# Gate tiles, gate sigmoids and stick-breaking heads placed elsewhere in the attention ticks of a two-block layer stack

## The reference, cut to what matters

```python
# block 1 (twice)
y_a = forgetting_attention(q_a, k_a, v_a, f_a + b_forget)      # 6 heads, "fox"
y_b = stick_breaking_attention(q_b, k_b, v_b)                  # 5 heads, "sb"
y_c = dsa_attention(q_c, k_c, v_c, q_i, k_i, w_i)              # 5 heads, "dsa": top 64 keys by 4 index heads
g_a, g_b, g_c = jnp.split(jax.nn.sigmoid(gates), 3, axis=-1)   # gates = part of h @ w_in, 3 x 1024 wide
x = x + (g_a * (y_a @ w_up_fox) + g_b * (y_b @ w_up_sb) + g_c * (y_c @ w_up_dsa)) @ w_out
# block 2 (twice)
mixed = jax.nn.sigmoid(gate_a) * y_swa_projected + jax.nn.sigmoid(gate_b) * y_moba_projected   # 8 + 8 heads
x = x + gt1 * (mixed @ w_out)
```

## Time and profile before

| | us |
|---|---|
| median of 3 runs (lowest, highest) | 2136.32 (2134.76, 2137.23) |
| the profiled execution's own time | 2141.54 |
| its span from first to last instruction | 2139.8 |
| PE busy in the span | 2025.4 (95%) |
| DVE busy | 1469.8 (69%) |
| ACT busy | 975.3 (46%) |
| mean granted TensorE clock | 0.950 of full |

### The profile page before, as it was taken

The page is one execution under the profiler, slowest core; times in us unless marked ns, Lnnn a source line. Parts: engine busy times, 40 slices in busy tenths (PEclk is TensorE's granted clock), DMA queues, the critical chain, the costliest instruction groups (busy, mean ns, idle before and its releaser), DMA issues.

```text
span 2139.8 us, 35812 instructions
## 1 busy us (share of the span) xinstructions
PE 2025.4 (95%) x13668; PEld 1862.9 (87%) x13668; DVE 1469.8 (69%) x2602; ACT 975.3 (46%) x1466; POOL 36.9 (2%) x72
## 2 busy tenths in 40 slices
PE   6999999889999999999989997998899979898998
PEld 6999998879999999998879996897799968887997
DVE  7776558677766776458578776765766668566665
ACT  5335455543344344455644344554444445534443
POOL 0000000000000000000000000000000000000000
PEclk9999999899998999999799998996899989989999
DMA  8774443257763774443247762531345544223453
GB/s 307 269 264 176 177 158 119 89 188 279 280 236 140 276 283 183 163 166 122 68 178 265 276 230 85 199 115 36 135 177 188 195 149 156 109 79 128 177 192 131
DMA packets 76906, 382.15 MB, mean 179 GB/s; under 512 B 8960, under 2 KB 9088, under 8 KB 55552
## 3 DMA queue, kind: packets, MB, share of 16 engines
q1 hardware_dynamic: 67392, 329.78, 42.6%
q0 software_dynamic: 9408, 50.90, 7.0%
HBM read 379.60 MB, written 1.05 MB: 178 GB/s over the span
## 4 chain that ended last, share of the span: by engine, by line
PE 84%; DVE 10%; ACT 4%; issue 2%; DMA 1%; SPq 0%; DVEq 0%; ACTq 0%
PE psum L544 26%; PE psum L545 26%; PE psum L546 26%; DVE weights_low_a L1315 2%; ACT weights_high_a L989 1%; PE psum L867 1%; PE psum L839 1%; DVE h_low L1366 1%; PE psum L637 1%; PE psum L752 1%; PE psum L841 1%; PE psum L635 1%; PE psum L840 1%; DVE weights_low_b L1315 1%; PE psum L743 1%
## 5 line engine op out<-in xcount | busy, mean ns | idle before, releaser
L544 PE MATMUL psum<-h_high,weights_high_a 128*128 128x256 f32 x2480 | 713.9, 288 | 14.6 <-DVE h_low L1362 6.5
L545 PE MATMUL psum<-h_low,weights_high_a 128*128 128x256 f32 x2480 | 706.2, 285 | 0.0
L546 PE MATMUL psum<-h_high,weights_low_a 128*128 128x256 f32 x2480 | 705.6, 285 | 0.0
L1315 DVE TENSOR_TENSOR weights_low_a<-raw_a,weights_high_a 128x2048 fp32r<-128x2048 f32 (+1 forms) x232 | 459.9, 1983 | 109.7 <-ACT weights_high_a L989 107.1
L544 PEld LDWEIGHTS psum<-h_high,weights_high_a 128*128 128x128 f32 x2480 | 479.5, 193 | 29.8 <-issue 12.2
L545 PEld LDWEIGHTS psum<-h_low,weights_high_a 128*128 128x128 f32 x2480 | 480.4, 194 | 7.1 <-issue 1.0
L546 PEld LDWEIGHTS psum<-h_high,weights_low_a 128*128 128x128 f32 x2480 | 479.7, 193 | 0.0
L989 ACT ACTIVATE weights_high_a<-raw_a 128x2048 fp32r<-128x2048 f32 (+1 forms) x232 | 386.8, 1667 | 163.5 <-PE psum L546 144.0
L1315 DVE TENSOR_TENSOR weights_low_b<-raw_b,weights_high_b 128x1024 fp32r<-128x1024 f32 x224 | 273.4, 1221 | 78.9 <-ACT weights_high_b L989 77.9
L989 ACT ACTIVATE weights_high_b<-raw_b 128x1024 fp32r<-128x1024 f32 x224 | 237.6, 1061 | 162.4 <-PE psum L546 162.4
L544 PE MATMUL psum<-weights_high_b,gated_high 128*128 128x512 f32 x608 | 241.1, 396 | 0.0
(11 more groups left out here) (283 smaller groups left out, 2848.0 us busy)
## 6 DMA issues: line engine op xcount, KB each, us to landing
ada_weights<-in_w_ada POOLq DMA_DIRECT2D x64, 768.0 KB, 5.0
raw_a<-in_w_ffn_a_a SPq DMA_DIRECT2D x44, 1024.0 KB, 6.7
raw_a<-in_w_ffn_b_a SPq DMA_DIRECT2D x44, 1024.0 KB, 6.9
raw_a<-in_w_ffn_a SPq DMA_DIRECT2D x64, 512.0 KB, 4.1
raw_b<-in_w_ffn_b SPq DMA_DIRECT2D x64, 512.0 KB, 3.4
raw_a<-in_w_proj_a SPq DMA_DIRECT2D x28, 1024.0 KB, 5.8
raw_a<-in_w_gate_a SPq DMA_DIRECT2D x26, 1024.0 KB, 4.9
raw_b<-in_w_ffn_a_b SPq DMA_DIRECT2D x44, 512.0 KB, 3.5
```

Source lines behind the costliest of these rows:

```text
L544: pe.matmul(out, l_hi, r_hi, start=start, stop=False, skip_group_check=True)
L545: pe.matmul(out, l_hi, r_lo, start=False, stop=False, skip_group_check=True)
L546: return pe.matmul(out, l_lo, r_hi, start=False, stop=stop, skip_group_check=True)
L1315: dve.tensor_tensor(wlo[kind][:, p, 0:width], raw[kind][:, p, 0:width], whi[kind][:, p, 0:width].bitcast(F32), ALU.subtract).then_inc(lo_r ...
```

## The change

Five things are changed.

1. Block 1 runs four stick-breaking heads at items 2, 3, 6 and 7; the six fox heads come after the index heads, the fifth stick-breaking head after them, the dsa heads stay last. The top-64 rounds move from ticks 10 to 15 to ticks 12 to 18, two rounds of the wide half at a time.
2. A table `GATE_TICKS` says in which tick a gate tile is made. In block 1 these are ticks 0 to 26 without 17, 19 and 23; in block 2 they are 0 to 10, 15, 17, 19, 21 and 23. Weight splits that went with a tick now go with the number of the gate tile.
3. The tanh of the gates and both table loads leave the ticks and stand at the start of ACT's up stage, with weight splits between them.
4. The split of the a part of the second up slot leaves the ticks as well: on ACT it stands behind the first tanh, on DVE ahead of the first merge.
5. DVE masks the new scores of item t before it finishes the y of item t-4.

```diff
 def schedule1():
-    items = [("ckv", 0), ("kv", 0), ("fox", 0), ("fox", 1), ("turn", 0), ("turn", 1)]
+    items = [("ckv", 0), ("kv", 0), ("sb", 0), ("sb", 1), ("turn", 0), ("turn", 1), ("sb", 2), ("sb", 3)]
     items += [("idx", h) for h in range(IDX)]
     items += [("turn", 2), ("turn", 3)]
-    items += [("fox", h) for h in range(2, FOX)]
-    items += [("sb", h) for h in range(SB)] + [("dsa", h) for h in range(DSA)]
+    items += [("fox", h) for h in range(FOX)]
+    items += [("sb", 4)] + [("dsa", h) for h in range(DSA)]
...
+GATE_TICKS = {1: [t for t in range(27) if t not in (17, 19, 23)],
+              2: list(range(11)) + [15, 17, 19, 21, 23]}
...
+                    if items[back][0] == "ckv":
+                        pe.wait_ge(now().forget_rows_ready, 2)
...
             def ticks(l, blk, items, gates, walk, n0):
-                first_tanh = len(items) + 3 - KD
...
-                for tick in range(max(len(items) + 3, gates)):
+                for tick in range(len(items) + 3):
+                    g = gate_of(blk, tick)
                     item_copy(blk, items, tick - 3)
                     stick_exp(items, tick - 1)
-                    if tick < gates and tick % 3 == 0:
-                        split_high(l, blk, 1, n0 + tick // 3 + 1)
+                    if g is not None and g % 3 == 0:
+                        split_high(l, blk, 1, n0 + g // 3 + 1)
...
-                    if tick < gates:
-                        gate_tile(blk, walk, tick, gates)
-                        if tick % 3 == 1 or (blk == 2 and tick == 15):
-                            split_high(l, blk, 0, n0 + tick // 3 + 2)
+                    if g is not None:
+                        gate_tile(blk, walk, g)
+                        if g % 3 == 1 and g < gates - 2:
+                            split_high(l, blk, 0, n0 + g // 3 + 2)
...
-                    if tick == first_tanh - 1:
-                        act.preload_act_table_set("exp_and_others")
-                    if first_tanh <= tick < first_tanh + KD:
-                        gate_tanh(blk, tick - first_tanh)
-                act.preload_act_table_set("natural_log_exp_and_others")
...
             def up_and_out(l, blk, n0):
-                for n in range(n0, n0 + 6):
+                act.preload_act_table_set("exp_and_others")
+                gate_tanh(blk, 0)
+                split_high(l, blk, 0, n0 + 1)
+                for f in (1, 2):
+                    gate_tanh(blk, f)
+                split_high(l, blk, 1, n0 + 1)
+                for f in (3, 4):
+                    gate_tanh(blk, f)
+                split_high(l, blk, 0, n0 + 2)
+                for f in (5, 6, 7):
+                    gate_tanh(blk, f)
+                act.preload_act_table_set("natural_log_exp_and_others")
+                for n in range(n0 + 1, n0 + 6):
...
             def ticks(l, blk, items, gates, n0):
-                for tick in range(max(len(items) + 4, gates + 1)):
+                for tick in range(len(items) + 4):
+                    g, before = gate_of(blk, tick), gate_of(blk, tick - 1)
                     item_late(items, tick - 1)
-                    item_y(blk, items, tick - 4)
                     if tick < len(items) and items[tick]:
                         item_early(blk, items, tick)
+                    item_y(blk, items, tick - 4)
...
                 1: {3: tokens1_latent,
-                    10: lambda: top_rounds(0, 3), 11: lambda: top_rounds(0, 3), 12: lambda: top_rounds(0, 2),
-                    13: lambda: top_rounds(1, 3), 14: lambda: top_rounds(1, 3),
-                    15: lambda: (top_rounds(1, 2), finish_selection())},
+                    12: lambda: top_rounds(0, 3), 13: lambda: top_rounds(0, 3), 14: lambda: top_rounds(0, 2),
+                    15: lambda: top_rounds(1, 2), 16: lambda: top_rounds(1, 2), 17: lambda: top_rounds(1, 2),
+                    18: lambda: (top_rounds(1, 2), finish_selection())},
...
                 g = g1 if blk == 1 else g2
+                split_low(l, blk, 0, n0 + 1)
```

More of the change, by code:

```diff
@@ L220, in schedule2, with gate_of @@
     return items
+GATE_TICKS = {1: [t for t in range(27) if t not in (17, 19, 23)],
+              2: list(range(11)) + [15, 17, 19, 21, 23]}
+def gate_of(blk, tick):
+    return GATE_TICKS[blk].index(tick) if tick in GATE_TICKS[blk] else None
 HEADS = ("fox", "sb", "dsa", "swa", "moba")
@@ L848, in ticks @@
                     pe.wait_ge(now().gain_copied, 2)
-                for tick in range(max(len(items) + 3, gates)):
-                    if tick < gates:
-                        gate_tile(l, blk, walk, tick)
+                for tick in range(len(items) + 3):
+                    g = gate_of(blk, tick)
+                    if g is not None:
+                        gate_tile(l, blk, walk, g)
                     if tick < len(items) and items[tick]:
@@ L1179, in item_copy, with gate_tile @@
                                ACT.Copy).then_inc(now().pt_copied, 1)
-            def gate_tile(blk, walk, tick, gates):
-                mark = walk.mark[tick]
+            def gate_tile(blk, walk, g):
+                mark = walk.mark[g]
                 act.wait_ge({"a": now().used[0], "b": now().used[1], "g": now().group_done}[mark[0]], mark[1])
-                act.activation((g1 if blk == 1 else g2)[:, tick, :], ps[:, tick % 2, 0:SEQ],
+                act.activation((g1 if blk == 1 else g2)[:, g, :], ps[:, g % 2, 0:SEQ],
                                ACT.Copy).then_inc(now().gate_copied, 1)
@@ L1602, in ticks @@
             def ticks(l, blk, items, gates, n0):
-                for tick in range(max(len(items) + 4, gates + 1)):
+                for tick in range(len(items) + 4):
+                    g, before = gate_of(blk, tick), gate_of(blk, tick - 1)
                     item_late(items, tick - 1)
-                    item_y(blk, items, tick - 4)
                     if tick < len(items) and items[tick]:
                         item_early(blk, items, tick)
-                    if tick < gates and tick % 3 == 0:
-                        split_low(l, blk, 1, n0 + tick // 3 + 1)
-                    before = tick - 1
-                    if 0 <= before < gates and (before % 3 == 1 or (blk == 2 and before == gates - 1)):
+                    item_y(blk, items, tick - 4)
+                    if g is not None and g % 3 == 0:
+                        split_low(l, blk, 1, n0 + g // 3 + 1)
+                    if before is not None and before % 3 == 1 and before < gates - 2:
                         split_low(l, blk, 0, n0 + before // 3 + 2)
```

6 lines of the change are left out of this document (3 added, 3 removed).

## The result

| | before | after |
|---|---|---|
| median of 4 runs (lowest, highest), us | 2135.54 (2133.36, 2137.23) | 2120.75 (2118.35, 2122.68) |
| span of the profiled execution | 2139.8 | 2116.7 |
| mean granted TensorE clock | 0.950 | 0.967 |

The ratio is 0.9933, 95% interval 0.9919 to 0.9948: 14.8 us faster, where 14.3 were forecast (2122 against 2136.32). So from here on stages are compared, each with its granted clock.

The account below looks back on a forecast made before the run. Bounds taken: PE work in block 1's ticks, small-step chains and low clock in block 2's last ticks. Block 1 +5, block 2 -24, block 1's clock +4.5 gave -14.5 us: 2122 on the median of 2136.32, range 2098 to 2137.

Parts of the forecast that it names:

- Block 2's ticks: Block 2's ticks: moving four gate tiles late gives -11.7 + 1.3 + 0.4 = -10.0 us a layer.
- the walk: Tick-by-tick reckoning with profiled durations: 12.8 us of PE waits in block 1's ticks, block 2's last stage about 32.5 us.
- Rival C: Block 2's last ticks: clock stays at 1.2 GHz because waits between late tiles hold it down; 2144 us, chance 0.10.
- four tiles enter the last ticks for 0.4 us: Block 2's last ticks: four added gate tiles nearly all fill PE waits, lengthening the stage by only 0.4 us.
- Rival E: Block 2's last ticks: late tiles lie on the chain, costing 2 of 2.93 us each; 2138 us, chance 0.15.
- Block 1's ticks: Block 1's ticks: 100.7 us work, 12.8 waits, 0.6 for the last y, 114.1 against 113.1: +1.0 us a layer.
- the term for the clock: Block 1: gaps in ticks 5 and 17 each bring a half-clock spell, three more in all at 1.5 us: +4.5.
- Rival B: Block 1's ticks: the new PE waits don't arise, ticks near 102 us; total 2095.5 us, chance 0.20.
- turn_y: The turn_y stage gets shorter through a higher clock: -0.5 us a layer in block 1, -0.7 in block 2.
- Block 2's up stage: Block 2's up stage starts at full clock, partly offset by the added split on DVE: -1.3 us a layer.
- Block 1's up stage: Block 1's up stage: the split ahead of DVE's first merge, where DVE is nearly the bound, adds +2.0 us a layer.
- rival D: Start of the four up stages: each table load delays the first merge another 1.28 us, 5.1 in all; 2127, chance 0.05.

## Why the prediction was right, and where it was not

**The total** was met, 2122 against 2120.75, and so was the course: faster. That it was met so closely is luck. Block 1 was forecast at +9.5 us (+5, and +4.5 for its clock), and between the two profiled executions it came out at -0.4; block 2 was forecast at -24 and came out at -27.7. The stages thus gave 28.1 us, about twice the 14.5 of the sum. Of these, 4.9 us were lost again in stretches that the change doesn't touch, and 8.4 us are the distance of the two profiled executions from their medians (6.0 above, 2.4 below): 28.1 - 4.9 - 8.4 = 14.8.

**Block 2's ticks** were forecast at -10.0 us a layer and measured -11.3 and -10.0; the waits that the walk found (1.9, 1.7, 1.5 us) were 1.52, 1.23 and 0.90, that of tick 11 was 1.13 (1.3), and the clock stayed at 1.00. Rival C is out. But the step "four tiles enter the last ticks for 0.4 us" failed as an account. It compared a stretch with tanhs with a stretch without them and booked the difference to the tiles. The runs split it: taking the tanhs, the loads and the slot split out brings 32.1 us at clock 0.59 down to 22.7 where the clock is full; four late tiles then cost 8.9. For layer one that is 47.9 - 58.7 = -10.8 before tick 15, then -9.4 and +8.9: -11.3. Against the same kernel without late tiles, where the clock holds, they bring 81.1 - 79.6 = 1.5 us a layer. Rival E had the price right, 2 of 2.9 us for a late tile; that it comes from the tile's place ahead of the scores, as E says, no run tested. Its 16 us did not show because parts 3 and 4 gave as much. The sentence that tanh and table load "also leave this stretch" was the main term, written as an aside; it should have been a term of its own, bounded by 0 and 7.5 us of ACT time plus the clock.

**Block 1's ticks**: forecast +1.0 and, for the clock, two spells a layer; measured +0.8 and -0.3 with two spells a layer (clock 0.97 of 113.9, 3.4 us). The walk's waits came where it put them: tick 5 with 0.60, 1.11 and 2.45 (1.05, 1.4, 2.9 forecast), tick 17 with 2.83 (3.2), tick 19 with 0.99 (1.6); tick 9 had 0.7 instead of 2.25. Idle of PE was 9.3 us, not 13.4. So the walk's waits were 4 us a layer too dear: with the term for the clock (+4.5) both layers' ticks were forecast at +6.5 together, and measured +0.6. The sum also took layer two for a copy of layer one, while before the change it was 1 us longer and at clock 0.93. And the term saw traded waits alone: the run with parts 3 and 4 alone has 110.6 and 108.6 us, -2.6 and -5.5, and what the rest of the change adds is +3.4 and +5.3. Rival B (the waits don't arise) is out.

**turn_y**: -0.5 and -0.7 forecast, -1.2 measured in all four layers. The term was undersized: in block 1 PE's busy part fell from 4.10 to 2.41 us, and 0.5 us of the 1.7 came back as waits. Block 2's up stage was undersized too, -1.3 forecast and -2.5 and -1.5 measured.

**Block 1's up stage**: +2.0 a layer forecast, +1.5 measured in layer one. The order on DVE was the predicted one, a split and only then the first merge:

```profile
408.20 2.29 DVE L1333 TENSOR_TENSOR weights_low_a<-raw_a,weights_high_a 128x2048 fp32r<-128x2048 f32 x1 [2.89 <-ACT weights_high_a L1001]
410.41 1.08 DVE L1809 SCALAR_TENSOR_TENSOR merge_terms<-gates_one,psum 128x256 f32<-128x256 f32 x3
```

The split began 2.8 us into the stage, not 4, and the first merge 5.0 us into it, where before it was 3.5 (409.28 behind 405.80), so most of the split lay in time in which DVE had waited for PE. The clock is not what makes the stage long: in layer two it takes the same 28.90 us at clock 1.00, and PE stands idle for DVE at its end.

```profile
1085.27 0.76 PE L553 MATMUL psum<-weights_high_a,h_high 128*128 128x512 f32 x1 [3.24 <-DVE weights_low_a L1333]
```

Against the kernel before layer two shows no difference (28.9 both), because there that kernel ran it at clock 0.94.

**The table load**, rival D. ACT at the start of the up stage:

```profile
403.79 0.42 ACT L1242 ACTIVATE y_high<-psum 128x256 fp32r<-128x256 f32 x1
404.22 1.28 ACT L1247 ACT_TABLE_LOAD   x1
405.52 0.84 ACT L1204 ACTIVATE gates_one<-gates_one 128x768 f32<-128x768 f32 x1
```

The load starts 0.01 us behind the copy before it and the tanh 0.02 us behind the load, so there is no second piece of 1.3 us on either side. The Trainium skill (ScalarE: Activation LUTs, What ACT_TABLE_LOAD costs) adds a drain of about 1.38 us to every switch of the table. This trace does not agree, and the measurement decides.

**What was not forecast at all**: the rest of the program, which the change doesn't touch, took 4.9 us more in the profiled execution of after, 3.9 of them in the two last stretches, whose clock was lower (0.94 and 0.95 instead of 0.95 and 0.98). I have no cause for it.

What stays open: how much of block 2's loss before is the clock and how much the queue, as two numbers. With the same ACT work the stretch took 32.1 us at 0.59 and at 0.69, which speaks for the queue, and so do the 3.8 us at a like clock. But without it, and with the slot split gone as well, the same kernel took 26.2 us at 0.78 and 22.7 at 1.00; and in these 22.7 us PE waits 6.8, as much as the 6.7 of the earlier trace rows, so by PE's busy time all of the 9.4 us between them is matmuls at the low clock. No run held the clock still.

## What to carry to other kernels

In a stretch where small steps chain PE, DVE and ACT, look at everything that stands in the queue of the engines beside PE, even if they are busy only two thirds of the time: moving 7.5 us of unrelated ACT work away bought as much as the whole change, partly by a shorter queue and partly by a higher clock. A forecast that meets the total has to be checked stage by stage: here errors of 10 and 4 us stood under a change of the total that was met to 0.5 us. When several edits meet in one stretch, price each against the stretch without the others, not the stretch before against the stretch after. And ask of filler work, that is work moved to where an engine waits, whether it hides: two kernels at the same clock, with and without it, tell at once (here 2.2 of 2.9 us were paid).

## What the runs showed of the hardware

The granted clock moves these stages more than the late tiles do. In block 2's ticks with two late tiles less, the two layers ran the same instructions in 83.6 us at clock 0.96 and 80.6 at 1.00, a difference larger than what the two tiles were worth. The untouched stretch from block 1's first out projection to its second ticks took 504 us at 0.97 in the kernel before, and 497 at 0.98 in the run with the tanhs alone moved: a single profile's span says little at the 0.3% level. The stretch in the kernel before:

```profile
433.15:937.29 504.14, 497.01 (x3361) 463.28 (x3361) 356.30 (x539) 213.17 (x249) 17.76 (x33) 0.97 0.62 225
```

And in the run with the tanhs and loads alone moved:

```profile
435.70:932.70 497.00, 489.69 (x3360) 455.90 (x3361) 356.25 (x539) 213.29 (x249) 17.84 (x33) 0.98 0.63 228
```

The busy time of DVE and ACT is the same to 0.2 us, and PE's differs by 7.3.
